# The delta heads' inversion: the transposed blocks by a third product per level instead of by transposes of the updated inverse

## The chip, the cores and the metric

The kernel runs on one core of one Trainium2 chip. The metric is the device time of one execution in microseconds (us), given as the median of several runs. Engines are named as the profile does: PE is TensorE (PEld its weight loads), DVE is VectorE, ACT is ScalarE, POOL is GpSimd, SP is the engine that issues the weight transfers.

## What is computed

One inference step of a decoder with two layers: layer 0 has gated DeltaNet heads (4) and retention heads (4), layer 1 has mLSTM heads (4), each layer followed by a squared-ReLU MLP. The input is a prompt of 1024 tokens and eight sample tokens, width 1024. The part that this document is about is the delta rule's triangular solve, per head and per chunk of tokens:

```python
kb = k * beta[..., None]
lower = jnp.einsum('nbhik,nbhjk->nbhij', kb, k) * decay_strict
a_mat = lower + jnp.eye(c, dtype=lower.dtype)
rhs = jnp.concatenate([v * beta[..., None], kb * jnp.exp(g)[..., None]], axis=-1)
sol = lax.linalg.triangular_solve(a_mat, rhs, left_side=True, lower=True)
u, w = sol[..., :dv], sol[..., dv:]
# a scan over the chunks follows: v_new = u_c - w_c s; o = ...; s = s * gl_c + kd_c^T v_new
```

`a_mat` is a unit lower triangular matrix. The kernel uses chunks of 128 tokens (the result doesn't depend on the chunk's length), so each head has eight matrices of 128x128, and it inverts them instead of solving.

## The kernel before

All matrices lie with 128 rows on the 128 partitions. The projections, the MLPs and the output projections are tiles of weights of 1024x128, split into a high and a low part, and each is 72 products of 128x128 on 128x344 on TensorE (L336). VectorE drains each third of a tile (L739, L772, L1217, L1232) and splits the weights that have arrived (L698, L700).

Each mixer head is a generator, on TensorE and on VectorE alike (`mixer_ab`), that yields at named places. `weave` runs it and at each place lays a number of steps of the next head's projections between; the numbers stand in `DELTA_FILL`. At the places `level 0`, `level 1`, `block` and `turn` the number is 0: nothing is laid in between during the inversion. At `invert` it is 2. Each engine runs its instructions in the order written, and they meet by semaphores: `to_pe` is raised by VectorE (`tell`, which first waits for VectorE's last counted instruction and then raises it), `full` says that a bank of the accumulator memory holds a result, `drained` that it may be written again (`claim` waits for it, `take` waits for `full`).

The inversion doubles the size of the inverted diagonal blocks level by level. E (`s[15]`) holds the inverse so far, Dm (`s[14]`) its transpose, LT (`s[12]`) the transposed strictly lower part, Pm (`s[11]`) a masked product. The eight chunks of a head go in two halves of four, and one instruction of VectorE covers one half. Level 0 is done by VectorE from masks (L946 to L959). For each level 1 to 6:

- `level` 0 and 1: TensorE makes LT-transposed times Dm for the four chunks of a half, into bank 0 or 1. VectorE masks the result into the even blocks of Pm (L966) and tells TensorE.
- `block`, for half 0 and 1: TensorE makes Pm-transposed times E into bank 3 or 1. VectorE subtracts the odd blocks from E (L974), waits for that and, except in level 6, tells TensorE.
- `turn`, for half 0 and 1, levels 1 to 5 only: TensorE transposes the updated E into bank 2 or 4 (`turned`, L388). VectorE copies the even blocks into Dm (L984), tells TensorE, and sets the blocks of Pm to zero that the next level must find empty (L988).

A product of 128x128 on 128x128 is written by `mm` (L391) and stands in the trace as two MATMUL records and two LDWEIGHTS records; a transpose is written at L388 and stands as one of each. After the last level the scan over the chunks follows (L995, L1000, L1004, L1009). All four delta heads come first, from about 137 us to about 590 us of the span, then four retention heads, then layer 0's output projection and MLP, and then layer 1.

Of the kernel before, what the change touches and what calls it, by code (L numbers as in the profile page):

```python
# [22 lines left out]
ALU = mybir.AluOpType  # L23
# [45 lines left out]


DELTA_FILL = {"start": 7, "conv q": 14, "conv k": 10, "conv v": 8, "norm": 4, "operands": 12, "invert": 2,
              "level 0": 0, "level 1": 0, "block": 0, "turn": 0, "scan": 1, "state": 1, "residual": 1, "values": 1,
              "sample": 2, "rows": 3, "output": 3, "outer": 0}
RETENTION_FILL = {"gate": 5, "rope q": 10, "rope k": 10, "operands": 10, "scan": 8,
                  "state": 4, "sample": 4, "rows": 5, "outer": 3, "output": 5}
# [84 lines left out]
def build(nc, io):  # L160
    with ExitStack() as ctx:
# [90 lines left out]
        def chunk(a, c, n=1):  # L252
            return a[:, c * C:(c + n) * C]
# [47 lines left out]
        def _(pe):  # L301
# [78 lines left out]
            def per_chunk(b, reader, half, f):  # L380

                claim(b, reader)
                for q in range(4):
                    last = f(MB[b][:, q * C:(q + 1) * C], 4 * half + q)
                publish(last, b)
# [4 lines left out]
            def mm(o, l, r, start=True, stop=True):  # L390
                return nc.tensor.matmul(o, l, r, start=start, stop=stop)  # L391
# [13 lines left out]
            def mixer_ab(s, h, delta):  # L405

                if delta:
                    over_partitions(sel(32 + h, 36), rows_a[0:36, :], "act")
                    yield "start"
                    over_partitions(sel(h, 36), rows_a[0:36, :], "dve")  # L410
                    yield "conv q"
                    yield "conv k"
                    yield "conv v"
                    for x in (10, 12):
                        yield "norm"
                        pe.wait_ge(*n.awaited(act_to_pe))
                        over_partitions(ones, s[x], "act")
                else:
                    yield "gate"
                    yield "rope q"  # L420
                    yield "rope k"
                q, k, v = (s[4], s[5], s[6]) if delta else (s[6], s[7], s[2])
                yield "operands"
                pe.wait_ge(*n.awaited(to_pe))
                for half in range(2):
                    turned(half, "dve", k, half)
                for half in range(2):
                    turned(2 + half, "dve", v, half)
                if delta:
                    for half in range(2):  # L430
                        per_chunk((4, 0)[half], "dve", half, lambda o, c: mm(o, chunk(k, c), chunk(s[14], c)))
                for half in range(2):
                    per_chunk(1 + half, "dve", half, lambda o, c: mm(o, chunk(k, c), chunk(q, c)))
                if delta:
                    LT, Pm, Dm, E = s[12], s[11], s[14], s[15]
                    for half in range(2):
                        yield "invert"
                        pe.wait_ge(*n.awaited(to_pe))
                        turned(half, "dve", LT, half)
                    for lv in range(1, LEVELS):  # L440
                        for half in range(2):
                            yield f"level {half}"
                            pe.wait_ge(*n.awaited(to_pe))
                            per_chunk(half, "dve", half, lambda o, c: mm(o, chunk(LT, c), chunk(Dm, c)))
                        for half in range(2):
                            yield "block"
                            pe.wait_ge(*n.awaited(to_pe))
                            per_chunk((3, half)[half], "dve", half, lambda o, c: mm(o, chunk(Pm, c), chunk(E, c)))
                        if lv < LEVELS - 1:
                            for half in range(2):  # L450
                                yield "turn"
                                pe.wait_ge(*n.awaited(to_pe))
                                turned((2, 4)[half], "dve", E, half)

                Kd, V, qg, QKT = s[16], s[17], s[10], s[13]
                yield "scan"
                pe.wait_ge(*n.awaited(to_pe))
                for c in range(NC_):
                    if c:
                        yield "state"  # L460
                        pe.wait_ge(*n.awaited(to_pe))
                    if delta:
                        claim(0, "dve")
                        publish(mm(MB[0][:, 0:P], chunk(k, c), S[:, 0:P]), 0)
                    claim(2, "act")
                    mm(MB[2][:, 0:C], S[:, 0:P], chunk(qg, c), True, False)
                    if delta:
                        yield "residual"
                        pe.wait_ge(*n.awaited(to_pe))
                        claim(1, "dve")  # L470
                        publish(mm(MB[1][:, 0:P], chunk(s[15], c), resid[:]), 1)
                        yield "values"
                        pe.wait_ge(*n.awaited(to_pe))
                    vv = vnew[:] if delta else chunk(V, c)
                    publish(mm(MB[2][:, 0:C], vv, chunk(QKT, c), False, True), 2)
                    claim(3, "dve")
                    publish(mm(MB[3][:, 0:P], chunk(Kd, c), vv), 3)

                yield "sample"
                pe.wait_ge(*n.awaited(to_pe))  # L480
                pe.wait_ge(state_in, n.awaited(state_in, 16)[1])
                claim(4, "dve")
                for b in range(NB):
                    mm(MB[4][:, 2 * b:2 * b + 2], s[9][:, b * P:(b + 1) * P], kq[:, b, :])
                publish(mm(MB[4][:, 2 * NB:3 * NB], ones, small[:, 0:NB]), 4)
                yield "rows"
                sample_outer([small[:, NB:2 * NB] if delta else samp[:, 0:NB]])

                yield "output"
                pe.wait_ge(*n.awaited(act_to_pe))  # L490
                over_partitions(ones, s[12], "act")
                yield "outer"
                pe.wait_ge(*n.awaited(to_pe))
                for half in range(2):
                    b = (3, 0)[half]
                    claim(b, "dve")
                    publish(mm(MB[b][:], krow[0:NB, :], s[13][0:NB, half * 512:(half + 1) * 512]), b)
# [168 lines left out]
        def _(v):  # L666
# [15 lines left out]
            def tell(sem):  # L682

                n.settle()
                v.sem_inc(*n.made(sem))  # L685
# [145 lines left out]
            def mixer_ab(s, h, delta, unit):  # L831
# [99 lines left out]
                if delta:  # L931
# [30 lines left out]
                    for lv in range(1, LEVELS):  # L962
                        for half in range(2):
                            ps = take(half)
                            mask = levels[:, lv, :].rearrange("p (n b) -> p n b", b=1 << lv)
                            tt_(even_blocks(chunk(Pm, 4 * half, 4), lv), even_blocks(ps[:], lv),  # L966
                                mask.unsqueeze(1).broadcast_to([P, 4, mask.shape[1], 1 << lv]), ALU.mult).then_inc(*done(half))
                            tell(to_pe)
                            yield "block"
                        for half in range(2):  # L970
                            b = (3, half)[half]
                            ps = take(b)
                            e = every_other(chunk(E, 4 * half, 4), lv, 1)
                            tt_(e, e, every_other(ps[:], lv, 1), ALU.subtract).then_inc(*done(b))  # L974
                            n.settle()
                            if lv < LEVELS - 1:
                                tell(to_pe)
                                yield "turn"
                        if lv < LEVELS - 1:
                            for half in range(2):  # L980
                                b = (2, 4)[half]
                                ps = take(b)
                                d = every_other(chunk(Dm, 4 * half, 4), lv, 0)
                                nc.vector.tensor_copy(d, every_other(ps[:], lv, 0)).then_inc(*done(b))  # L984
                                tell(to_pe)

                                left = chunk(Pm, 4 * half, 4).rearrange("p (n x y b) -> p n x y b", x=2, y=2, b=1 << lv)
                                nc.vector.memset(left[:, :, 1, 0, :], 0.0)  # L988
                                yield f"level {half}"
# [783 lines left out]
```

## Time and profile before

| | |
|---|---|
| three timed runs | 2943.44 us median, 2941.95 to 2946.55 |
| the profiled execution | 2947.95 us |
| its span, first to last instruction | 2946.2 us |
| mean granted clock of TensorE | 0.978 |
| TensorE busy | 2837.9 us, 96% of the span |
| VectorE busy | 1648.9 us, 56% |
| ScalarE busy | 354.7 us, 12% |

The page of the profile gives shares over the whole span. The chain of waits follows the work that ended last back from the last instruction; in order of time it shows what a stretch of the span was made of. The order of time of all instructions shows what lies beside it, and in square brackets how long an engine idled before an instruction and which instruction released it. The granted clock is 1.00 at 2.4 GHz and 0.50 at 1.2 GHz. A matmul's duration is from its issue to its modelled end, so a train of them is shorter than the sum of the durations.

### The profile page before, as it was taken

How to read it: one execution, taken by the hardware profiler on the slowest of the kernel's cores; microseconds unless marked ns; L12 is line 12 of the kernel's file. 1: busy time of each engine (PE TensorE's matmuls, PEld its weight loads, DVE VectorE, ACT ScalarE, POOL GpSimd, SP SyncE). 2: the span in 40 equal slices, each digit the busy share in tenths (PEclk: the TensorE clock that was granted, in tenths of full speed). 3: DMA queues.
4: the chain of work that ended last, by engine and by line, in shares of the span. 5: the costliest groups of instructions: out<-in, count | busy, mean ns of one | idle time of the engine just before them, and what ended most of it. 6: DMA issues, size and time to landing. Idle time of an engine off the chain costs nothing.

```text
span 2946.2 us, 42340 instructions
## 1 busy us (share of the span) xinstructions
PE 2837.9 (96%) x17818; PEld 2723.0 (92%) x17818; DVE 1648.9 (56%) x3052; ACT 354.7 (12%) x598; POOL 23.2 (1%) x25
## 2 busy tenths in 40 slices
PE   7998989999999999999999999999999999999997
PEld 6878878799889999999999999998899999999997
DVE  6657667566667536354366535456576355363554
ACT  4202213021221000000001111112130000000001
POOL 3000000000000000000000000000000000000000
PEclk9999999999999999999999999999999999999999
DMA  3100001021121111111112112022111111111111
GB/s 112 41 16 29 31 21 37 14 82 52 52 104 44 43 51 44 51 44 51 44 51 90 58 47 60 29 60 67 65 67 44 51 43 51 44 51 43 51 44 72
DMA packets 42685, 150.99 MB, mean 51 GB/s; under 512 B 5768, under 2 KB 7688, under 8 KB 41488
## 3 DMA queue, kind: packets, MB, share of 16 engines
q1 hardware_dynamic: 30528, 111.20, 11.9%
q10 hardware_dynamic: 11984, 37.22, 3.4%
q8 instruction: 141, 2.31, 0.3%
q14 instruction: 32, 0.26, 0.0%
HBM read 130.32 MB, written 18.08 MB: 50 GB/s over the span
## 4 chain that ended last, share of the span: by engine, by line
PE 75%; DVE 5%; issue 1%; ACT 1%; DMA 0%; ACTq 0%; DVEq 0%; SPq 0%
PE proj L336 66%; PE bank L391 7%; PE bank L378 1%; PE bank L388 1%; DVE x_lo L784 0%; PE bank L597 0%; DVE w_lo L700 0%; DVE s L739 0%; DVE w_hi L698 0%; DVE h L1374 0%; DVE s L900 0%; DVE s L899 0%; DVE s L898 0%; DMA w_raw<-w_all 0%; DMA s<-retention 0%
## 5 line engine op out<-in xcount | busy, mean ns | idle before, releaser
L336 PE MATMUL proj<-x_hi,w_hi 128*128 128x344 f32 x4788 | 1577.3, 329 | 21.9 <-DVE x_lo L784 8.3
L336 PE MATMUL proj<-x_lo,w_hi 128*128 128x344 f32 x4788 | 1542.5, 322 | 0.0
L336 PE MATMUL proj<-x_hi,w_lo 128*128 128x344 f32 x4788 | 1542.3, 322 | 0.0
L336 PEld LDWEIGHTS proj<-x_hi,w_hi 128*128 128x128 f32 x4788 | 912.5, 191 | 50.2 <-issue 37.8
L336 PEld LDWEIGHTS proj<-x_lo,w_hi 128*128 128x128 f32 x4788 | 913.0, 191 | 2.8 <-issue 0.9
L336 PEld LDWEIGHTS proj<-x_hi,w_lo 128*128 128x128 f32 x4788 | 912.2, 191 | 0.0
L1232 DVE TENSOR_TENSOR h<-h,proj 128x344 f32<-128x344 f32 x144 | 73.9, 513 | 372.2 <-PE proj L336 372.2
L700 DVE TENSOR_TENSOR w_lo<-w_raw,w_hi 128x1024 fp32r<-128x1024 f32 x202 | 247.5, 1225 | 7.0
L1217 DVE TENSOR_TENSOR mlp_t<-proj,rbc 128x344 f32<-128x344 f32 x192 | 99.0, 516 | 237.6 <-PE proj L336 223.9
L391 PE MATMUL bank<-s,s 128*128 128x128 f32 x1408 | 193.9, 283 | 9.2 <-DVE s L959 8.4
L391 PEld LDWEIGHTS bank<-s,s 128*128 128x128 f32 x1408 | 173.8, 195 | 14.9 <-DVE s L959 10.0
L1413 ACT ACTIVATE ssq<-h 128x344 f32<-128x344 f32 x15 | 7.1, 482 | 1271.1 <-DVE h L772 1271.1
L698 DVE CAST w_hi<-w_raw 128x1024 fp32r<-128x1024 f32 x202 | 138.7, 687 | 1.3 <-ACT ssq L1413 0.6
L739 DVE TENSOR_TENSOR s<-proj,rbc 128x344 f32<-128x344 f32 x156 | 78.5, 513 | 101.5 <-PE proj L336 98.4
L1222 DVE TENSOR_TENSOR x_lo<-mlp_u,x_hi 128x344 fp32r<-128x344 f32 x192 | 99.4, 518 | 6.5
L1219 DVE SCALAR_TENSOR_TENSOR mlp_u<-mlp_t 128x344 f32<-128x344 f32 x192 | 99.4, 518 | 6.6
L1221 DVE CAST x_hi<-mlp_u 128x344 fp32r<-128x344 f32 x192 | 65.3, 340 | 6.5
L1413 ACT ACTIVATE sq_third<-h 128x344 f32<-128x344 f32 x105 | 50.8, 484 | 142.8 <-DVE h L772 138.0
L1502 ACT ACTIVATE s<-bank 128x128 f32<-128x128 f32 x64 | 17.8, 278 | 414.4 <-PE bank L391 414.4
L388 PE MATMUL bank<-consts,s 128*128 128x128 f32 x416 | 56.8, 276 | 9.1 <-DVE s L904 4.2
L772 DVE TENSOR_TENSOR h<-h,proj 128x344 f32<-128x344 f32 x48 | 24.6, 512 | 68.9 <-PE proj L336 68.6
L388 PEld LDWEIGHTS bank<-consts,s 128*128 128x128 f32 x416 | 46.3, 141 | 16.0 <-DVEq L685 9.3
(266 smaller groups left out, 1754.0 us busy)
## 6 DMA issues: line engine op xcount, KB each, us to landing
w_raw<-w_all SPq DMA_DIRECT2D x204, 512.0 KB, 3.4
h<-x SPq DMA_DIRECT2D x8, 516.0 KB, 9.3
h<-x ACTq DMA_DIRECT2D x8, 516.0 KB, 6.5
h_spill<-h ACTq DMA_DIRECT2D x8, 516.0 KB, 2.7
h<-h_spill ACTq DMA_DIRECT2D x8, 516.0 KB, 6.4
y<-h ACTq DMA_DIRECT2D x8, 516.0 KB
sample_C<-state_c ACTq DMA_DIRECT2D x4, 1024.0 KB, 4.9
s_state_c<-sample_C ACTq DMA_DIRECT2D x4, 1024.0 KB
```

Source lines behind the costliest of these rows:

```text
L336: last = nc.tensor.matmul(PJ[:, tt, 0:TT], w[slot][:, k, :], x[:, k, tt * TT:(tt + 1) * TT], start=(at == 0 and j == 0), stop=(at == len(o ...
L388: per_chunk(b, reader, half, lambda o, c: nc.tensor.transpose(o, chunk(src, c), ident))
L391: return nc.tensor.matmul(o, l, r, start=start, stop=stop)
L698: nc.vector.tensor_copy(hi[:], src).then_inc(w_hi_done, 1)
L700: tt_(lo[:], src, hi[:].bitcast(F32), ALU.subtract).then_inc(w_split, 1)
L739: return tt_(third(dst, tt), ps, third(rbc, tt), ALU.mult)
L1217: drain(t, tt, lambda ps, tt: tt_(T_third[:], ps, third(rbc, tt), ALU.mult), g)
L1219: step(stt(U_third[:], T_third[:], 0.0, T_third[:], ALU.max, ALU.mult))
L1221: step(nc.vector.tensor_copy(hi, U_third[:]))
L1222: tt_(lo, U_third[:], hi.bitcast(F32), ALU.subtract).then_inc(x_ready, 1)
L1232: drain(t0 + 8 + c, tt, lambda ps, tt: tt_(hh, hh, ps, ALU.add), g)
L1413: act(third(SQT if at else SSQ, tt), hh, ACT.Square).then_inc(sq_made, 1)
```

## The change

At levels 1 to 5 the `turn` place and its transposes are gone. In `block` TensorE makes, for each half, a product more, E-transposed times Pm, into the bank that the transpose used (2 or 4), ahead of Pm-transposed times E. VectorE subtracts its even blocks from Dm (the subtraction takes the place of the copy), tells TensorE, and then subtracts the other product from E as before. The transpose of E - Pm-transposed E is Dm - E-transposed Pm, so the mathematical result is the same. The memset of Pm's blocks comes behind E's subtraction. Banks, masks and the other levels stay.

```diff
-              "level 0": 0, "level 1": 0, "block": 0, "turn": 0, "scan": 1, "state": 1, "residual": 1, "values": 1,
+              "level 0": 0, "level 1": 0, "block": 0, "scan": 1, "state": 1, "residual": 1, "values": 1,
...
                         for half in range(2):
                             yield "block"
                             pe.wait_ge(*n.awaited(to_pe))
+                            if lv < LEVELS - 1:
+
+                                per_chunk((2, 4)[half], "dve", half, lambda o, c: mm(o, chunk(E, c), chunk(Pm, c)))
                             per_chunk((3, half)[half], "dve", half, lambda o, c: mm(o, chunk(Pm, c), chunk(E, c)))
-                        if lv < LEVELS - 1:
-                            for half in range(2):
-                                yield "turn"
-                                pe.wait_ge(*n.awaited(to_pe))
-                                turned((2, 4)[half], "dve", E, half)
...
                         for half in range(2):
+                            if lv < LEVELS - 1:
+                                b = (2, 4)[half]
+                                ps = take(b)
+                                d = every_other(chunk(Dm, 4 * half, 4), lv, 0)
+                                tt_(d, d, every_other(ps[:], lv, 0), ALU.subtract).then_inc(*done(b))
+                                tell(to_pe)
                             b = (3, half)[half]
                             ps = take(b)
                             e = every_other(chunk(E, 4 * half, 4), lv, 1)
                             tt_(e, e, every_other(ps[:], lv, 1), ALU.subtract).then_inc(*done(b))
                             n.settle()
                             if lv < LEVELS - 1:
-                                tell(to_pe)
-                                yield "turn"
-                        if lv < LEVELS - 1:
-                            for half in range(2):
-                                b = (2, 4)[half]
-                                ps = take(b)
-                                d = every_other(chunk(Dm, 4 * half, 4), lv, 0)
-                                nc.vector.tensor_copy(d, every_other(ps[:], lv, 0)).then_inc(*done(b))
-                                tell(to_pe)
```

## Rows read from the trace of the kernel before

**Rows 1.** The page: span, busy time of the engines, the chain that ended last.

```profile
span 2946.2 us, 42340 instructions
PE 2837.9 (96%) x17818; PEld 2723.0 (92%) x17818; DVE 1648.9 (56%) x3052; ACT 354.7 (12%) x598; POOL 23.2 (1%) x25
...
PE 75%; DVE 5%; issue 1%; ACT 1%; DMA 0%; ACTq 0%; DVEq 0%; SPq 0%
```

**Rows 2.** The chain in order of time, head 3's inversion: start us, us, what.

```profile
523.85 3.77 PE bank L391 x32
527.62 0.02 issue
527.64 0.43 DVE s L974
528.07 0.03 issue
528.10 0.06 DVEq L685
528.16 0.04 issue
528.21 0.66 PE bank L388 x4
528.86 3.77 PE bank L391 x32
```

**Rows 3.** Order of time, one level of head 3; in brackets idle before, releaser.

```profile
524.52 0.17 DVE L988 MEMSET s<- 128x128 f32 x1 [0.20 <-DVE s L984]
524.96 0.43 DVE L966 TENSOR_TENSOR s<-bank,levels 128x256 f32<-128x256 f32 x1 [0.28 <-PE bank L391]
...
526.75 0.42 DVE L974 TENSOR_TENSOR s<-s,bank 128x256 f32<-128x256 f32 x1 [0.47 <-PE bank L391]
...
527.44 0.60 PE L388 MATMUL bank<-consts,s 128*128 128x128 f32 x4
527.64 0.42 DVE L974 TENSOR_TENSOR s<-s,bank 128x256 f32<-128x256 f32 x1 [0.47 <-PE bank L391]
```

**Rows 4.** Groups by line, all of the span: count, busy us, mean ns, idle.

```profile
L984 DVE COPY s<-bank 128x256 f32<-128x256 f32 x40 | 16.0, 399 | 3.5 <-DVE s L974 3.5
```

**Rows 5.** Order of time, first levels of heads 0, 1 and 3.

```profile
148.48 0.43 DVE L966 TENSOR_TENSOR s<-bank,levels 128x256 f32<-128x256 f32 x1 [0.20 <-PE bank L391]
150.17 0.43 DVE L966 TENSOR_TENSOR s<-bank,levels 128x256 f32<-128x256 f32 x1 [1.26 <-PE bank L391]
...
155.27 0.42 DVE L966 TENSOR_TENSOR s<-bank,levels 128x256 f32<-128x256 f32 x1
...
271.92 0.43 DVE L966 TENSOR_TENSOR s<-bank,levels 128x256 f32<-128x256 f32 x1 [0.26 <-PE bank L391]
273.83 0.43 DVE L966 TENSOR_TENSOR s<-bank,levels 128x256 f32<-128x256 f32 x1 [1.49 <-PE bank L391]
...
518.52 4.08 PE L391 MATMUL bank<-s,s 128*128 128x128 f32 x32 [2.10 <-DVE s L959]
...
519.79 0.42 DVE L966 TENSOR_TENSOR s<-bank,levels 128x256 f32<-128x256 f32 x1 [0.19 <-PE bank L391]
```

**Rows 6.** Stretches: length, engines' busy time, granted clock, DMA share, GB/s.

```profile
148.00:152.00 4.00, 4.00 (x22) 3.84 (x21) 1.25 (x4) 0.00 (x0) 0.00 (x0) 0.58 0.00 0
519.79:544.99 25.20, 24.39 (x202) 22.44 (x203) 13.69 (x40) 0.00 (x0) 0.00 (x0) 1.00 0.01 2
...
144.00:180.00 36.00, 32.63 (x251) 29.85 (x250) 20.09 (x56) 0.00 (x0) 0.00 (x0) 0.95 0.00 1
552.00:606.00 54.00, 49.22 (x280) 42.19 (x279) 31.25 (x60) 13.40 (x19) 0.00 (x0) 0.94 0.20 70
```

**Rows 7.** Waits: who for whom, us in total, times, longest.

```profile
ACT s L1471 <- DMA p_state_a<-state: 6.3, 1, 6.3
DVE mix L834 <- DMA s<-retention: 3.2, 1, 3.2
```

## The prediction

> **What bounds the kernel now.** I read the page's busy shares first, then its chain of waits. TensorE is busy 96% of the span, VectorE 56%, and 75% of the chain that ended last is TensorE's [rows 1]. The reader is to see there that time on TensorE, or time in which it waits for somebody, is what counts; VectorE matters only where TensorE waits for it. A share over the span doesn't say this of the inversion, so the second view is the chain in head 3's inversion [rows 2]. It repeats every 5.01 us (523.85, 528.86): 3.77 us of products, one subtraction on VectorE (L974), the hand-over of 0.03+0.06+0.04 us, and 0.66 us of four transposes. So a level is part TensorE at full rate, part a round trip to VectorE. The third view, the order of time in one level [rows 3], shows what lies beside the chain: the first half's four transposes at 527.44 run while VectorE does the second half's subtraction (527.64), and TensorE then stands until 528.21. The copies of the transposes (L984), the memsets (L988) and the next level's masking (L966) all lie beside TensorE's products. No projection is laid into these places (their fills are 0), so a level's length goes into the span one to one: TensorE and VectorE are both in it and nothing else goes on.
>
> **What one product costs.** In [rows 3] VectorE is released by the four groups of products in turn, the first at 524.96, the third at 526.75, the last at 527.64 (the second stands between): 2.68 us for three groups of four, 0.893 a group, 0.2233 us a product (two MATMUL records each: x32 for 16). The 3.77 us of the chain are 16 x 0.2233 = 3.57 and 0.20 until the last result can be read. With 0.02 before VectorE starts, a group's result is read 0.22 us after its last product has been issued.
>
> **What the change removes.** In five of the six levels (1 to 5) of four heads, so in 20 levels (L984 stands 40 times, once a half [rows 4]): eight transposes, two waits of TensorE, two copies of 0.40 us and two hand-overs on VectorE. Of a level's 5.01 us this takes everything but the products: 5.01 - 3.57 = 1.44 us.
>
> **What it adds.** Eight products a level, stationary E and moving P, 128x128 on 128x128 like the other sixteen. The trace of before has this shape in the same place, but not these two operands. The low bound is that they run like the transposes, whose group of four (527.44 to the end at 528.04) has one record each: 0.60 less a record's 0.27 is 0.33 for three, 0.11 us apiece; the high bound is a product in a stretch at half clock, a group of four in 1.69 us (148.48 to 150.17 [rows 5]), 0.42 apiece. I take 0.2233, the row of the same shape at full clock. So 8 x 0.2233 = 1.79 us a level. The ends would make a level 0.56 shorter (-11 us in all) or 1.9 longer (at full clock there is no cause for that); since type, shape, engine and neighbours are the same, I give the low end 1 in 100, within the fourth rival's share, and the high end nothing beyond the slow stretches that are there already. The copy of 0.40 becomes a subtraction from the same kind of bank; I take L974's 0.42.
>
> **Do the hand-overs hide?** The new order on TensorE is L0 L1 X0 B0 X1 B1 (L = L-transposed times D, X = the new product, B = the old block product, digit = half), six groups of 0.893. I set L0's start at 0.
> - X0 needs the masked P of half 0: L0 done 0.89, readable 1.11, L966 0.42, hand-over 0.13 (L974's end at 528.07 to TensorE at 528.21 in [rows 2], less the rounding) = 1.66. TensorE arrives at 1.79. It fits by 0.1, and this step is the same as in the kernel before, where the chain runs through all four groups without a gap [rows 2].
> - VectorE must be free for it at 1.11. It takes the previous B1 at 0.22, subtracts to 0.64, settles and does the memset of 0.17, until about 0.9 (a memset starts 0.20 after a copy's end in [rows 3]). It fits by 0.2.
> - The next L0 needs D of half 0: X0 done 2.68, readable 2.90, told at 3.45, wanted at 5.36. D of half 1: X1 done 4.47, told at 5.24, wanted at 6.25.
> - B0's subtraction comes behind D0's on VectorE (3.32 and a settle) and is readable at 3.79: no clash. B1's: D1 is finished and told at 5.24, B1 readable at 5.58.
> - The next L1 writes bank 1, which B1 also used: free at 5.58 + 0.42 + 0.13 = 6.13, wanted at 6.25. It fits by 0.1.
> So nothing is queued behind a late wait; TensorE is the bound of a level all through, where before it was it for only part. A level takes 24 x 0.2233 = 5.36 us. If the cover were gone, two of these fits would fail first (P of half 0 and bank 1), both with 0.1 us to spare. The bounds for all hand-overs together are 0 and what stood exposed before beside the last transposes, 0.45+0.13 = 0.58 us a level.
>
> **The sum.** 5.36 - 5.01 = +0.35 us a level, 20 levels: +7.0 us. Level 6 has no transposes and keeps its length; the first level's entry (setup on VectorE, TensorE idle 2.1 us before 518.52 [rows 5]) stands ahead of the changed steps. In head 0 the first period is 6.79 us and not 5.17 as in head 3 (L966 at 148.48 and 155.27, against 519.79 and 524.96 [rows 3, 5]); head 1's two maskings lie 1.91 us apart, head 0's 1.69, since TensorE's granted clock is 0.58 from 148 to 152, that is, mostly its lower level of 1.2 GHz [rows 5, 6]. That surcharge of 1.6 us is a stretch of time at 1.2 GHz with TensorE at work in it in both kernels; it neither grows nor shrinks with what TensorE does. The profiled execution took 2947.95 us (span 2946.2, 1.75 around it), so it becomes 2954.9. The median of the three timed runs, 2943.44, lies 4.5 below it; the same +7.0 gives 2950.4, my forecast.
>
> **Against the sum: the clock.** Through the changed levels of head 3, with transposes as 8 of 40 records a level, the granted clock is 1.00 [rows 6]. The Trainium skill ("TensorE: Matmul & The Clock Gate", Part 4: PE-mode transpose) says a transpose doesn't count as busy for the clock gate as a matmul does. By that rule swapping transposes for products could only keep the clock up. The trace shows the levels at full clock with transposes in them, so the rule has nothing to give there; what it could still give is the third rival.
>
> **The rivals.**
> 1. *The hand-overs show.* The two fits of 0.1 us are worked out from sums of rows with 0.02 in each. If VectorE's order D0, B0, memset, D1, B1, memset, P0 slips, TensorE waits every level. For it: three operations of 0.42, 0.17 and 0.42 us must be served in the 1.7 us between B1's end and X0. Against it: VectorE has 0.28 and 0.47 us of idle ahead of each of these now [rows 3]. Price: 0.1 to 0.58 us a level, +2 to +12, so 2952.4 to 2962; with 0.25 us a level 2955.4.
> 2. *The delay is swallowed.* Some later wait of the head may end at a time that doesn't move. For it: VectorE once waits 3.2 us for the retention table, ACT once 6.3 us for a store [rows 7]. Against it: both transfers are issued on progress of this chain, and the others it waits for are TensorE's and VectorE's own steps. At most 3.2 of the 7.0: +3.8, 2947.2.
> 3. *The clock holds at the entries.* If real products keep it up in heads 0 and 1's first levels, 2 x 1.6 us come back: +3.8, 2947.2. Against it: the clock fell at 148.5 in the very first products, before any changed step of that head.
> 4. *The other side: less slow clock between the inversions.* Each head starts later by 1.75 us more than the one before, so the places in which TensorE idles before a head's operands and inversion fall differently against the stretches at half clock. From 144 to 606 the granted clock is 0.92 to 1.00 by stretch (0.95 in the first); (1 - clock) x length sums to 21.9 us over the eight stretches whose first and last stand in [rows 6], which is what the slow stretches cost at most. From a third of them (7.0 us) on, the change is no slower. Half of them gone would give -4, 2939.5. For it: the stretches differ from head to head (0.95, 0.96, 1.00, 1.00 in the inversions). Against it: a shift has no sign; it is as likely to add them.
>
> **How the numbers follow.** Forecast 0.72, rival 1 0.10, rival 2 0.05, rival 3 0.06, rival 4 0.07 (of which 0.04 below no change and the rest between). A measurement of this kernel can tell about 0.2%, 5.9 us, from no change; three runs spread over 4.6 us. The forecast's own range is +4 to +10 by that scatter and by slow stretches that come or go, so about a quarter of it falls within 0.2%. Slower: 0.72 x 0.74 + 0.10 = 0.63. Same: 0.19 + rivals 2, 3 and half of 4, 0.33. Faster: 0.04. The range takes in rivals 2 and 3 at the low end and half a hand-over a level of rival 1 at the high one: 2945.5 to 2956.
>
> **What would show it.** Right: the starts of the masking (L966 before) repeat every 5.36 us, L391's chain runs through from the first level to the sixth with neither VectorE nor transposes in it, VectorE idles more than 0.4 us ahead of most of its groups, and 160 MATMUL records of L388 are gone against 320 more of L391. Handing over late would show as idle time of TensorE ahead of L391 with VectorE as its releaser. The prediction is wrong if a level takes under 5.1 us (then a product with E and P costs less than 0.2233), or if levels take 5.36 us and the span doesn't grow by about 7 (then the clock column or a later wait took it back).

## The result

Over 16 executions of each kernel, beside each other, the changed kernel takes 2949.86 us (2942.76 to 2955.21) and the kernel before 2943.02 us (2937.66 to 2947.06). The ratio is 1.0023, 95% interval 1.0016 to 1.0030: slower by 6.8 us, where 7.0 was forecast (2950.4). Two later comparisons of the same pair gave 1.0033 (1.0020 to 1.0046) and 1.0028 (1.0016 to 1.0039), that is 9.7 and 8.2 us by the ratios. The changed kernel also scatters more: the standard deviation of one execution is 3.3 us over its 28, against 1.7 us over the 46 of the kernel before.

The profiled execution after took 2949.07 us with a span of 2947.3, that of before 2947.95 with 2946.2. These two differ by 1.1 us only, so one pair of profiles can't carry the result: the stages have to be compared. The page after, to be held against [rows 1]:

```profile
span 2947.3 us, 42580 instructions
PE 2843.4 (96%) x17978; PEld 2737.7 (93%) x17978; DVE 1651.1 (56%) x3052; ACT 354.5 (12%) x598; POOL 23.2 (1%) x25
```

TensorE has 160 matmuls more (17978 - 17818): 320 records of products came and 160 of transposes went. The chain of waits in order of time, in head 3's inversion after, shows what became of [rows 2] (start us, us, what):

```profile
518.90 0.28 DVE s L957
519.19 0.04 issue
519.23 30.89 PE bank L391 x272
```

From the first level to the last, 272 records in a row are TensorE's own: five levels of 48 and a sixth of 32. VectorE's subtraction, its hand-over and the transposes are no longer in it. 136 products x 0.2233 = 30.37 us; the rest is the 0.20 until the last result can be read, and 0.32 in the first level, mostly its wait for the second memset, which was there before too (the first level's products took 4.09 us in the chain before and not 3.77). In order of time one level looks like this (idle before in brackets; L964 masks P, L973 subtracts from D, L978 from E, L983 is the memset), against [rows 3]:

```profile
531.38 0.42 DVE L964 TENSOR_TENSOR s<-bank,levels 128x256 f32<-128x256 f32 x1 [0.21 <-PE bank L391]
532.28 0.42 DVE L964 TENSOR_TENSOR s<-bank,levels 128x256 f32<-128x256 f32 x1 [0.47 <-PE bank L391]
533.17 0.42 DVE L973 TENSOR_TENSOR s<-s,bank 128x256 f32<-128x256 f32 x1 [0.47 <-PE bank L391]
534.06 0.42 DVE L978 TENSOR_TENSOR s<-s,bank 128x256 f32<-128x256 f32 x1 [0.47 <-PE bank L391]
534.58 0.17 DVE L983 MEMSET s<- 128x128 f32 x1
534.96 0.42 DVE L973 TENSOR_TENSOR s<-s,bank 128x256 f32<-128x256 f32 x1 [0.21 <-PE bank L391]
535.85 0.42 DVE L978 TENSOR_TENSOR s<-s,bank 128x256 f32<-128x256 f32 x1 [0.47 <-PE bank L391]
536.36 0.17 DVE L983 MEMSET s<- 128x128 f32 x1
536.74 0.42 DVE L964 TENSOR_TENSOR s<-bank,levels 128x256 f32<-128x256 f32 x1 [0.21 <-PE bank L391]
```

VectorE is released every 0.89 us and is idle ahead of every one of the six operations, so it is late for none. 536.74 - 531.38 = 5.36 us a level, and the levels behind the first are 5.36 apart in all four heads; before they were 5.01, but for the second of heads 0 and 1 (5.13 and 5.07). The first takes 5.52 us at full clock, and 5.17 before: 0.35 more as well. The 0.47 us of idle time ahead of VectorE's operations is in [rows 3] too; what is new is that TensorE has none of its own behind the first level.

The stretches (length, busy us of PE, PEld, DVE, ACT, POOL, granted clock, DMA share, GB/s) of the changed kernel: head 3's inversion, then head 3's scan, and head 0's scan:

```profile
520.50:547.50 27.00, 27.00 (x243) 27.00 (x244) 14.37 (x41) 0.00 (x0) 0.00 (x0) 1.00 0.00 1
547.46:578.72 31.26, 28.83 (x178) 24.14 (x177) 12.47 (x33) 2.17 (x8) 0.00 (x0) 0.95 0.06 18
171.28:201.36 30.08, 27.57 (x178) 22.56 (x177) 12.47 (x34) 2.17 (x8) 0.00 (x0) 1.00 0.07 18
```

and head 3's scan before:

```profile
545.00:575.06 30.06, 27.58 (x178) 22.55 (x177) 12.47 (x34) 2.17 (x8) 0.00 (x0) 1.00 0.05 18
```

TensorE is busy for all of the inversion, at full clock. The scan, which the change doesn't touch, takes 30.1 us where the clock is 1.00 and 31.3 where it is 0.95. This is the second thing that differs between the two profiles. From a head's first masking to its last state update, four heads together:

| profile | four inversions and scans, us | of it by slow clock, first levels | scans |
|---|---|---|---|
| before | 224.4 | 3.3 | 0.0 |
| before, second profile | 222.6 | 1.5 | 0.0 |
| after | 232.5 | 0.7 | 3.7 |
| after, second | 232.6 | 0.7 | 3.8 |
| after, third | 233.9 | 3.3 | 2.5 |

(The slow clock's part is each length less the one with clock 1.00: 26.96 us after and 25.21 before for an inversion, from its first masking to the first of level 6, and 30.07 for the rest.) Without the slow clock the four heads take 221.1 us in both profiles before and 228.1 in all three after: 7.0 us, which is 20 x 0.35. Slow stretches add 1.5 to 3.3 us before and 4.4 to 5.8 after. Those in the scans lie between the third and the fourth state update, which are then about 4.4 us apart and not 3.15. The changed kernel has one there in eight of its twelve scans, the kernel before in none of eight; doubling the third product, leaving it out or making the transposes four times (below) gives none in four scans each, and the two kernels below that copy on ScalarE, with shorter levels, have it in two of four each. So it isn't a longer level as such that brings them; why they fall there stays open. From head 3's last state to the last one of the retention heads it goes the other way, 251.3 and 251.1 us before, 249.6, 249.8 and 249.9 after. And head 0's first masking comes at 148.5 and 145.6 us before, at 144.3, 144.6 and 148.2 after: start-up alone differs by 4 us between executions of one kernel. That is why the first pair of spans is only 1.1 us apart: 8.1 us more in the four heads, 4.2 less ahead of them, 1.7 less up to the last retention head, and about 1 less in the rest.

### The profile page after: what moved, and what is told of

The parts are those of the page before. It is cut to its first block, busy times and chain, and to the rows that moved or that the text cites. A ratio compares the mean times of both kernels' runs of the same rounds, so it can differ in the third digit from the quotient of the medians.

```text
span 2947.3 us, 42580 instructions
## 1 busy us (share of the span) xinstructions
PE 2843.4 (96%) x17978; PEld 2737.7 (93%) x17978; DVE 1651.1 (56%) x3052; ACT 354.5 (12%) x598; POOL 23.2 (1%) x25
## 4 chain that ended last, share of the span: by engine, by line
PE 76%; DVE 5%; issue 1%; ACT 1%; DMA 0%; ACTq 0%; DVEq 0%
PE proj L336 67%; PE bank L391 7%; PE bank L378 1%; PE bank L388 0%; DVE x_lo L782 0%; DVE w_lo L698 0%; PE bank L595 0%; DVE s L737 0%; DVE w_hi L696 0%; DVE h L1369 0%; DVE s L897 0%; DVE s L898 0%; DVE s L896 0%; DMA s<-retention 0%; DVE s L913 0%
## 5 line engine op out<-in xcount | busy, mean ns | idle before, releaser
L391 PE MATMUL bank<-s,s 128*128 128x128 f32 x1728 | 222.7, 279 | 9.1 <-DVE s L957 8.4
L391 PEld LDWEIGHTS bank<-s,s 128*128 128x128 f32 x1728 | 206.4, 193 | 11.9 <-DVE s L957 9.8
L1123 DVE SCALAR_TENSOR_TENSOR state<-state,s,bank 128x257 f32<-128x257 f32 x32 | 15.5, 483 | 76.3 <-PE bank L391 76.1
L391 PE MATMUL bank<-s,state 128*128 128x128 f32 x256 | 49.8, 276 | 0.7 <-DVEq L683 0.7
```

## The experiments

**The changed kernel again.** No edit.

> The changed kernel once more, beside the others. Theory (TensorE is full in every level, 24 products of 0.2233 us against 5.01 us before): +7.0 us on the kernel before, maskings 5.36 us apart. Rival (the time goes to late hand-overs): the same sum, but idle time of TensorE ahead of the products. Rival (slow stretches of TensorE's clock): the maskings 5.36 apart, the difference to before anywhere from 0 to +14.

1.0033 (1.0020 to 1.0046) and maskings 5.36 us apart in all heads. From 521 to 545 us TensorE has no idle time ahead of a product. The rival of late hand-overs is out.

> The changed kernel beside the two others, once more: +7.0 us on the kernel before, that is a ratio of 1.0024, with its maskings 5.36 us apart.

1.0028 (1.0016 to 1.0039), 5.36 again. Profiles of one and the same kernel have the slow stretches in other places: here heads 0 and 1's first levels took 7.14 and 7.15 us, in the run before it 5.52 and 6.20.

**The third product twice.**

```diff
-per_chunk((2, 4)[half], "dve", half, lambda o, c: mm(o, chunk(E, c), chunk(Pm, c)))
+per_chunk((2, 4)[half], "dve", half, lambda o, c: [mm(o, chunk(E, c), chunk(Pm, c)) for _ in range(2)][1])
```

> The changed kernel with the third product made twice into the same bank (same result). Theory (TensorE is the bound of a level and nothing later takes it back): eight products more, 8 x 0.2233 = 1.79 us a level, 7.15 us a level, +36 us on the changed kernel, +43 on the kernel before. Rival (a later wait swallows part of a delay in the inversion, which would have made the change cheaper than its levels): levels of 7.15 us and clearly less than 36 us in the span.

2983.79 us, 1.0138 (1.0123 to 1.0154) of before, so +40.6 on the kernel before, and +34 on the changed kernel's median of the first comparison (the changed kernel did not run beside it). Levels 7.15 us apart (7.14 and 7.15), as forecast. The chain in head 3:

```profile
543.44 39.82 PE bank L391 x352
```

39.82 - 30.89 = 8.93 us for five levels, 1.79 a level. So the third product costs 0.2233 us apiece, and what the levels add arrives in the time: 40.6 of 43 expected, with an interval of 4.6 us to either side. No large part of it is swallowed later; this run alone would not tell a loss of 3 us.

**Without the third product.** The product's line is left out on TensorE, and VectorE takes D's blocks from the bank of the other product, ahead of E's, so D's new blocks are not the inverse's:

```diff
-                                per_chunk((2, 4)[half], "dve", half, lambda o, c: mm(o, chunk(E, c), chunk(Pm, c)))
...
-                                b = (2, 4)[half]
-                                ps = take(b)
-                                d = every_other(chunk(Dm, 4 * half, 4), lv, 0)
-                                tt_(d, d, every_other(ps[:], lv, 0), ALU.subtract).then_inc(*done(b))
-                                tell(to_pe)
                             b = (3, half)[half]
                             ps = take(b)
+                            if lv < LEVELS - 1:
+                                d = every_other(chunk(Dm, 4 * half, 4), lv, 0)
+                                tt_(d, d, every_other(ps[:], lv, 0), ALU.subtract).then_inc(*n.stepped())
+                                tell(to_pe)
```

> The changed kernel without the third product: D is updated from the bank of the other product, so its blocks are not those of the reference, and so is what follows from them. Theory: TensorE has 16 products, 3.57 us, and now hand-overs show: D of half 1 comes behind E of half 0 and is told at about 4.66, E of half 1 has left bank 1 at 5.25 - 3.57 = 0.8 us after the point at which the next L1 would want it. A level of 4.3 to 4.4 us, so -20 us on the changed kernel and not -36. Rival (products alone count): 3.57 us a level, -36 us on the changed kernel.

2928.89 us, 0.9958 (0.9943 to 0.9972), 24 us less than the changed kernel beside it. Levels are 4.30 us apart and not 3.57. From its chain, VectorE's half of a level and the products behind it:

```profile
510.48 0.43 DVE s L973
510.91 0.08 issue
511.00 0.17 DVE s L978
511.16 0.29 DVE s L970
511.45 0.03 issue
511.48 0.02 DVEq L680
511.50 0.09 issue
511.59 0.43 DVE s L973
512.02 0.14 issue
512.15 2.04 PE bank L391 x16
```

With eight products fewer the chain is VectorE's for half a level (L970 subtracts from D, L973 from E). So the hand-overs are real and set the level's length as soon as TensorE's work shrinks; in the changed kernel they are covered by the products that make it slower. Removing 1.79 us of TensorE's work a level returned 1.06.

**E before D on VectorE.**

```diff
-                            if lv < LEVELS - 1:
-                                b = (2, 4)[half]
...
-                                tell(to_pe)
                             b = (3, half)[half]
                             ps = take(b)
                             e = every_other(chunk(E, 4 * half, 4), lv, 1)
                             tt_(e, e, every_other(ps[:], lv, 1), ALU.subtract).then_inc(*done(b))
+                            if lv < LEVELS - 1:
+                                b = (2, 4)[half]
...
+                                tell(to_pe)
```

> The changed kernel, but VectorE takes each half's product for E first and the one for D behind it, so D of half 1 is told at 5.58 + 0.42 + 0.04 + 0.42 + 0.13 = 6.6 us after the level's start instead of 5.24, and TensorE wants it at 6.25. Theory (hand-overs hide up to the slack that I worked out): 0.35 us a level of waiting, a level of 5.7 us, +7 us on the changed kernel. Rival (the slack is larger than worked out, TensorE's queue runs on): a level stays at 5.36 us.

2953.38 us, 1.0033 (1.0021 to 1.0044): no more than the changed kernel beside it, 2953.21, where +7 was forecast. But the levels are 5.63 us apart, 0.27 more:

```profile
546.84 0.42 DVE L972 TENSOR_TENSOR s<-s,bank 128x256 f32<-128x256 f32 x1 [0.67 <-PE bank L391]
547.18 0.41 DVE L977 TENSOR_TENSOR s<-s,bank 128x256 f32<-128x256 f32 x1
547.71 1.42 PEld L391 LDWEIGHTS bank<-s,s 128*128 128x128 f32 x12 [0.20 <-DVEq L683]
547.80 0.17 DVE L983 MEMSET s<- 128x128 f32 x1 [0.20 <-DVEq L683]
```

TensorE's next loads wait for VectorE (L977's end at 547.59, 547.71). I had put 0.04 us between the two subtractions; without a wait between them the second starts 0.08 before the first ends (547.18 against 547.26). That takes 0.12 us off the forecast wait of 0.35, a little more than the 0.08 that are missing. The slack as such is about right: 1.0 us between told and wanted was forecast for D of half 1, and the wait for the later product together with the operation ahead of it uses it up. Since trace and time disagreed, it ran again:

> VectorE takes the product for E first, once more and with more rounds: its levels stood 5.63 us apart and not 5.36, but its time was that of the changed kernel. Theory (levels add up one to one and the first comparison was too coarse): 20 x 0.27 = +5.4 us on the changed kernel beside it. Rival (some of a delay in the levels is taken back in a head's later stages): under +2.5 us.

2955.5 us, 1.0039 (1.0026 to 1.0053), against 2951.84 and 1.0028 beside it: +3.7 us, where the levels (5.63 and 5.64 again) give +5.4. The intervals of the two ratios overlap, so this pair alone settles nothing. The stages say more. From a head's first masking to its last state update, the four heads together take 234.5 us in the first profile of this kernel, 0.9 of it by slow clock, and 240.2 us in the second, 6.6 by slow clock, all of it in first levels. Without the slow clock it is 233.6 us both times, 5.5 more than the changed kernel's 228.1. So up to the end of the scans nothing of the delay is swallowed. The slow stretches of these two profiles differ by 5.7 us, more than the +0.2 or the +3.7 is off the +5.4. So the two comparisons need not contradict the levels; that the slow stretches made the difference isn't shown, with one profile each.

**Half by product, half by transposes.** Half 1 as in the changed kernel, half 0 as before, and TensorE's order such that each wait has a group of products in front of it (TensorE's lines alone, the names of the groups added, the waits and VectorE's part left out):

```diff
...
+per_chunk(3, "dve", 0, lambda o, c: mm(o, chunk(Pm, c), chunk(E, c)))      # B0
...
+per_chunk(4, "dve", 1, lambda o, c: mm(o, chunk(E, c), chunk(Pm, c)))      # X1
...
+turned(2, "dve", E, 0)                                                     # T0
+per_chunk(1, "dve", 1, lambda o, c: mm(o, chunk(Pm, c), chunk(E, c)))      # B1
```

> Half 1 gets its transposed blocks from the product with E and P, half 0 from transposes, and TensorE's order in a level is L0 L1 B0 X1 T0 B1: the transposes stand behind X1, which covers the subtraction from E that they wait for, and B1 covers the copy into D. Theory: a level is 20 products and 4 transposes with no wait, 20 x 0.2233 + 4 x 0.109 = 4.90 us; against 5.36 that is -9.2 us over 20 levels, against the kernel before (5.01) -2.2 us. D of half 0 is told by 4.88 and wanted at 4.90, so up to 0.05 us a level may show. Rival (hand-overs set the length of a level, not TensorE's work): the third hand-over of half 0 shows as before, a level of 5.2 us or more, +4 us or more on the kernel before.

2943.20 us, 1.0003 (0.9994 to 1.0011). Levels 4.98 us apart and not 4.90. The change's cost is gone (1.0033 beside it, the intervals don't touch), with the product still in half of the places. What was forecast to fit by 0.02 us did not: once a level, where the next L0 starts, the gap from one product's record to the next is 0.19 us and not 0.11 (530.12 to 530.31). D of half 0 comes late: VectorE's word is there at 530.02, and TensorE's weight load starts at 530.09, 0.08 behind its place:

```profile
529.39 4.54 PE bank L391 x40
533.93 0.44 PE bank L388 x4
534.37 2.64 PE bank L391 x23
```

20 products and 0.44 of transposes are 4.91 us; from 529.39 to 534.37 it is 4.98. So of the 2.2 us that were to be won on the kernel before the levels leave 0.6, less than can be told. An order that covers both waits and keeps all eight transposes, 4.45 us of TensorE's work a level, wasn't tried.

**Every transpose four times**, in the kernel before.

```diff
-turned((2, 4)[half], "dve", E, half)
+per_chunk((2, 4)[half], "dve", half, lambda o, c: [nc.tensor.transpose(o, chunk(E, c), ident) for _ in range(4)][3])
```

> The kernel before with each transpose made four times into the same bank (same result), so that 32 transposes stand beside 16 products in a level. Theory: they fill both waits, a level is 16 x 0.2233 + 32 x 0.109 = 7.06 us, +2.05 a level and +41 us, and the granted clock of these levels stays 1.00. Rival (transposes do not count as activity for the clock): the granted clock falls below 1.00 in the levels, and they take more than 7.06 us.

2988.34 us, 1.0151 (1.0132 to 1.0169), +45 us, the forecast +41 being inside the interval. Levels 7.06 and 7.07 apart. Its chain, and the stretch of its head 3's levels:

```profile
553.24 3.49 PE bank L453 x32
556.74 3.57 PE bank L391 x32
560.31 3.49 PE bank L453 x32
```

```profile
558.00:586.00 28.00, 28.00 (x256) 28.00 (x255) 11.22 (x33) 0.00 (x0) 0.00 (x0) 1.00 0.01 1
```

32 transposes take 3.49 us, 0.109 each, and 16 products 3.57, with no wait between. So a transpose costs 0.49 of a product, and the eight of the kernel before were 0.87 us of work in 1.44 us of a level: 0.56 us was waiting. The granted clock stays 1.00 with TensorE in transposes for half of the time.

**The copies into D on ScalarE**, in the kernel before; TensorE waits for the bank to be drained instead of for VectorE's word, and VectorE's own copy and word are gone.

```diff
-turned((2, 4)[half], "dve", E, half)
+turned((2, 4)[half], "act", E, half)
...
+act(every_other(chunk(s[14], 4 * half, 4), lv, 0), every_other(ps[:], lv, 0), ACT.Copy).then_inc(*done(b))
```

> The kernel before with transposes in both halves, but ScalarE copies them into D instead of VectorE, and TensorE waits for the copy by the bank's own semaphore. Theory (before the change a level was 16 products and 8 transposes, 4.45 us of TensorE, plus 0.38 us for VectorE's subtraction and 0.18 us because D of half 0 queues behind it on VectorE): the 0.18 goes, the 0.38 stays, a level of 4.8 us, -0.2 a level and -4 us on the kernel before, -11 on the changed one. Rival (ScalarE's copy from a bank of 256 numbers takes longer than VectorE's 0.40 and D of half 0 is late again): 5.0 us a level and no change.

2941.02 us, 0.9990 (0.9981 to 0.9999), 2.1 us less by the medians where the levels give 20 x 0.18 = 3.6 and 4 was forecast; the interval holds all three. Levels 4.83 us apart. The chain of one level:

```profile
523.25 3.59 PE bank L391 x32
526.84 0.02 issue
526.87 0.43 DVE s L977
527.30 0.03 issue
527.32 0.06 DVEq L688
527.38 0.04 issue
527.43 0.66 PE bank L388 x4
528.08 3.59 PE bank L391 x32
```

The 0.18 between the transposes and the next products is gone (3.77 in [rows 2] is 3.59 here) and the wait for E stays. This answers where the kernel before lost its 0.56: 0.18 in waiting for the copy into D, which on VectorE came behind E's subtraction (it starts 0.17 after that ends, and here about with it), and 0.38 in the trip for E. The run changes the engine and the semaphore together, so how much of the 0.18 each gave isn't parted.

**And without the second semaphore.** On top of the last, TensorE waits for E, and in the scans for the residual, the values and the state, by the bank's own semaphore; VectorE's `tell` goes in these places.

```diff
-pe.wait_ge(*n.awaited(to_pe))
+pe.wait_ge(drained["dve"][b], n.n["fdve" + str(b)])
```

> The kernel in which ScalarE copies into D, and in which TensorE also waits for VectorE's subtraction from E, and in the scans for the residual, the values and the state, by the bank's own semaphore and not by a second one that VectorE raises after it (0.06 us on its queue and 0.07 around it in the chain before). Theory (a level is TensorE's work plus the exposed hand-over of E; in a delta scan only the state's hand-over is exposed, 7 a head): 0.08 us less at each, levels of 4.75 us and scan steps of 3.07 instead of 3.16, (20 + 28) x 0.08 = -4 us on that kernel, -6 to -8 on the kernel before. Rival (the second semaphore costs nothing, the time is the wait's own): levels of 4.83, no change.

2931.70 us, 0.9957 (0.9943 to 0.9970): -11.4 us on the kernel before and the fastest of those that compute the whole step. But not as expected. The levels stand 4.82 apart, no gain:

```profile
515.88 3.59 PE bank L395 x32
519.47 0.03 issue
519.50 0.02 DVEq L678
519.52 0.05 issue
519.57 0.43 DVE s L981
520.00 0.04 issue
520.04 0.66 PE bank L392 x4
```

The word to TensorE costs 0.04 and not 0.13, and VectorE starts its subtraction 0.10 after the products and not 0.02. In the scans the steps are 3.03 us apart and not 3.16; there the state's trip is covered by the projection step and leaves the chain:

```profile
545.19 0.48 PE proj L336 x3
545.67 0.68 PE bank L395 x4
```

A scan from first to last state is 22.99 us and not 23.85 where no slow stretch falls in it, 3.4 us for four heads, and the levels give 3.8 (20 x 0.19). That is 7.2 of 11.4 with an interval of some 4 us either side. The retention scans, which the edit touches too, are no shorter (17.97 us from first to last state for 17.89). No view I read shows where the rest would be, or whether there is one, and it stays open.

**The kernel before, a second profile.**

> The kernel before, a second profile, to see what its own executions differ in. Theory: the levels 2 to 5 of every head are 5.01 us apart again; the slow stretches of the clock lie in other places, and the first level of each head takes 5.17 us without one and about 6.8 with one.

2943.01 us. The levels behind the first are 5.00 to 5.01 apart, but for the second of heads 0 and 1, 5.13 and 5.06 (5.13 and 5.07 in the first profile); the first periods are 5.92, 5.18, 5.75 and 5.18 (6.79, 6.64, 5.17 and 5.17 in the first profile). The forecast 6.8 is thus no fixed surcharge: what a slow stretch costs depends on how much of it falls on TensorE's work.

## Why the prediction was right

- *What bounds a level.* Right. TensorE with two trips to VectorE before, TensorE alone after: the chain went from seven pieces a level to one of 30.89 us over six levels.
- *The price of the product.* 0.2233 us was taken from the same shape; the doubled product gives (39.82 - 30.89) / 40 = 0.2233. The ends (0.11 and 0.42) did not come up. The prediction's split of the chain's 3.77 us into 3.57 and 0.20 hid a wait: with the copies on ScalarE the same piece is 3.59. From the last product's issue to its reading it is 0.20 in both (527.44 to 527.64 in [rows 3]), but the piece begins at the transposes' modelled end, when products are already being issued (at 528.77 and not 528.86), and in the kernel before the wait for D makes up for what this leaves out. Neither the product's price, which comes from VectorE's releases, nor the 1.44 hangs on that split.
- *What the removed part was worth.* 1.44 us a level, with 0.87 of transposes (0.109 each by the fourfold transposes) and 0.56 of waiting, of which 0.18 was the wait for the copy into D (gone when ScalarE copied) and 0.38 the trip for E. The change bought 1.44 us for 1.79.
- *The hand-overs hide.* Right: VectorE idles 0.21 or 0.47 ahead of all six operations. The narrow ones, by 0.1 us, held. The same kind of sum was off by 0.08 in two experiments, in either direction (levels with E first 5.63 for 5.7, the half-and-half 4.98 for 4.90). So a fit of 0.1 held with little to spare, in part by luck, and one of 0.02 didn't. For the fit of VectorE the prediction's own rows gave a memset's end at 1.0 and not 0.9 (0.64 + 0.20 + 0.17); the trace has the memset 0.09 after the subtraction's end, not 0.20, so 0.9 and the spare 0.2 came out right all the same (0.21 idle ahead of L964).
- *The sum.* 20 x 0.35 = 7.0 by the trace, 6.8 us by 16 runs of each. That the two are 0.2 apart is luck in part: the other comparisons gave 9.7 and 8.2. One of the prediction's own signs of being wrong came up in the first pair of profiles, levels of 5.36 us and a span that grew by 1.1 only; it was start-up and the clock, as the stages show, and no later wait.
- *The slow clock* was put in as a surcharge that neither grows nor shrinks. It isn't fixed: in the kernel before it was 1.6 us in head 0's first level once and 0.75 the other time, and in the changed kernel 0 twice and 1.6 once, while scans that had none before had 2.5 to 3.8 us of it.
- *Rival 1* didn't occur; *rival 2* (swallowed later, +3.8) lies outside the interval of the first comparison, +4.7 to +8.8. The first of the two waits that it named is as long as before, 3.2 and 2.9 us before and 3.0, 2.9 and 3.0 after (`DVE mix L832 <- DMA s<-retention: 3.0, 1, 3.0`); ScalarE's, 6.3 us before, is 5.3 after. *Rival 3*, the clock held at the entries: two of three profiles after have no or little surcharge in head 0's and head 1's first levels (5.52 and 6.2 us), but the third has 7.14 and 7.15, and head 1's 5.18 of the second profile before shows that it can be missing without the product too. So the product doesn't hold the clock. The Trainium skill's sentence that a transpose doesn't count for the gate as a matmul does ("TensorE: Matmul & The Clock Gate", Part 4: PE-mode transpose) would have spoken for that rival; with half of TensorE's time in transposes the clock stayed 1.00, so here it makes no difference, and whether transposes alone would hold the clock no run shows.
- *Rival 4*, the slow stretches moved: they did, from the first levels into the scans. They cost 1 to 4 us more in these stages after than before, and what lies between head 3's last state and the last of the retention heads is 1.4 us shorter, so the net is not the gain that this rival priced. Three profiles against two can't say how much of that is the change and how much the scatter. The three comparisons, weighted by their intervals, give about 7.6 us with 1.6 to either side; next to the levels' 7.0 that leaves at most some 2 us for it, and shows none.

## What to carry to other kernels

Before an operation of half the price is replaced by one of the full price to get rid of a wait, write the round as two sums, TensorE's work and the trip, and compare them: here work went from 4.45 to 5.36 us to remove 0.56 of waiting. A wait is cheaper to cover than to buy off: giving the copies to the idle ScalarE took 0.18 of it for nothing, and interleaving the halves, with half of the products turned back into transposes, took back what the change had cost. Where a level is full on one engine, its length is here exact to 0.01 us and its effect on the time can be read off by multiplication, while one pair of whole profiles here differed by 1.1 us for a true difference of 7.

## What was not expected of the hardware

- Two operations of VectorE on banks, with no wait between, start 0.34 us apart and last 0.42 each (546.84 and 547.18); with a settle and a raised semaphore between them the next starts 0.14 to 0.20 after the end (511.45 to 511.59 without the third product, and the memset of [rows 3]).
- Letting TensorE wait for the subtraction's own semaphore saved 0.09 us behind it and cost VectorE 0.08 ahead of it (520.00 to 520.04, and 519.47 to 519.57), so that nothing was gained in the levels, while the same edit took 0.13 us off each scan step.
- Head 0 reached its first masking between 144.3 and 148.2 us in three profiles of the changed kernel, and a first level took 5.52 to 7.15 us for the same instructions (5.17 to 6.79 before). The level's part goes with where the clock was at 1.2 GHz; start-up's wasn't taken apart.
